# A gated linear recurrence on one Trainium2 core: scores of two levels made behind one chunk

## The chip, the cores and the metric

The kernel runs on one core of a Trainium2 chip. Its engines are TensorE (PE, matmuls; its weight loads are listed apart as PEld), VectorE (DVE), ScalarE (ACT), GpSimd (POOL) and SyncE (SP, which here issues the DMAs). Each runs its own instruction stream; streams are ordered only by semaphores. The metric is the device time of one execution in microseconds (us). The kernel before takes 2609.4 us (median of 3 runs, 2609.22 to 2610.02).

## The reference, cut to what matters

Two transformer blocks over 256 tokens of width 2048. The change touches the mixer of the first, a gated linear recurrence in both directions over 8 heads of width 128, beside a short convolution:

```python
proj = einsum('bsd,de->bse', rmsnorm(x), w_in)          # 8 pieces of 1024 columns
q_pre, fz_f, fz_b, i_pre, gate, b_gate, c_gate, h_conv = split(proj)
# per head, forward and, on flipped rows, backward (log_f: log of the forget gate, k = 1 - f):
#   S_t = diag(f_t) S_{t-1} + k_t v_t^T ;  o_t = S_t^T q_t
o = rmsnorm(o_fwd + o_bwd) * silu(gate)
y_conv = b_gate * conv3(c_gate * h_conv)
x = x + concat(o, y_conv) @ w_out
```

## The kernel before, in words

**Chunks.** Every large product streams its weights in chunks of 256 rows by 512 columns. SP loads a chunk to `raw` (a ring of 4), ACT rounds it to `hi` (L309), DVE makes the rest `lo` = `raw` - `hi` (L315), and PE multiplies it in 12 matmuls of 128x512 (L328 to L330) for two token tiles. A load waits for the `lo` four chunks before, a `hi` for PE's end of the chunk four before. PE's accumulators are two banks pairs, `acc[:, 0]` and `acc[:, 1]`; eight chunks make one block of 512 columns, which ACT then reads out (`act_scaled`, L735).

**The recurrence** runs inside 96 such chunks, in four groups of two heads (`GROUPS`), 24 chunks each (`RC`), three blocks a group: chunks 0-7 and 8-15 both into `acc[:, 0]`, 16-23 into `acc[:, 1]`. The order of everything is written by hand: each engine has a loop over g and k (`act_rec`, `dve_rec`, `pe_rec`), and steps are hung behind its own chunk k. ACT reads block 0 out behind its chunk 9 and block 1 behind its chunk 17; PE waits for the first before its chunk 8 (L1168).

**The levels.** Instead of a scan the kernel makes the 128x128 score matrix of each head and token tile in `ST` = 8 levels. Level s covers pairs of positions whose distance is decided in halves of 2^s rows. For each level:

- DVE `dve_decay(g, s)`: two products of 128x512 into `h_kd[s % 2]` and `h_qd[s % 2]` (L1001, L1003). It waits until the scores of level s - 2 are made. `dve_widen` (two more, L1009, L1011) prepares the factors of the next level, for s < 7.
- PE `scores(g, s)`: four products of 128x128 in f32, recorded as 8 matmuls (L1131), into `aux[:, s % 2]`. It waits for the decays of level s, and for the copy that empties its bank: for s = 2 to 6 the masked copy of level s - 2 by DVE (`a`), for s = 7 ACT's copy of level 5 (`kept`), for s = 0 and 1 ACT's copies of the group before.
- Copies into the matrix `h_a`: levels 0 to 4 by DVE (`dve_keep`, L989, a copy under a mask), 5 to 7 by ACT (`act_keep`, L915, L907).

PE then multiplies the matrix with the values (`output`, L1149, L1151, 16 records of 128x128) behind chunk 21 (in the last group behind 23). The same streams hold, for the next group, ACT's gate functions behind chunk 16 and keys behind 19, DVE's keys behind 17 (L962, L966) and gates behind 19 (L973), and, in the last group, the convolution (`pe_conv`, `act_conv`, `dve_conv`, L1229).

**Where the steps stand before.** PE: scores of level s behind its chunk 5 + 2s (5, 7, ..., 19). DVE: decays behind its chunks 6, 7, 9, 11, 13, 15, 16, 18, masked copies behind 8, 10, 12, 14, 16. ACT: copies of levels 5, 6, 7 behind 19, 21, 23.

Of the kernel before, what the change touches and what calls it, by code (L numbers as in the profile page):

```python
# [105 lines left out]
def build_program(nc, a, out):  # L106
    V, A, T = nc.vector, nc.scalar, nc.tensor
    with ExitStack() as ctx:
# [182 lines left out]
        g = 0  # L291
# [11 lines left out]
        def act_chunk(act, c, i, per, n=NB):  # L303

            k = c % RING
            act.wait_ge(raw_ready[k], i * (per // RING * 16) + 16 * (c // RING) + 16)
            if c >= RING or later(i):
                act.wait_ge(chunk_used, i * per + c - RING + 1)
            A.activation(hi[:, k, :, 0:n], raw[:, k, :, 0:n], ACT.Copy).then_inc(hi_ready, 1)  # L309
# [529 lines left out]
        DVE_KEEPS = 5  # L839
# [13 lines left out]
        def rec_chunk(g, k):  # L853
            return CH["in1b"] + RC * g + k
# [28 lines left out]
        def act_rec_readout(act, n):  # L883
            c0, func = REC[n // 3][n % 3]
            act.wait_ge(chunk_used, CH["in1b"] + 8 * (n + 1))
            act_scaled(act, c0, acc[:, 1 if n % 3 == 2 else 0], func).then_inc(h_sem["blk"], 1)
# [17 lines left out]
        def act_keep(act, g, s):  # L904
            act.wait_ge(h_sem["s"], g * ST + s + 1)
            if s == LEVELS:
                A.activation(h_c[:], aux[:, s % 2], ACT.Copy).then_inc(h_sem["kept"], 1)  # L907
                return
            act.wait_ge(h_sem["a"], (g + 1) * DVE_KEEPS)
            h = 1 << s  # L910
            for b in range(P // (2 * h)):
                for r, c in ((2 * b, 2 * b + 1), (2 * b + 1, 2 * b)):
                    rows_, cols_ = slice(r * h, (r + 1) * h), slice(c * h, (c + 1) * h)
                    dst = h_a[rows_].rearrange("p (x n) -> p x n", x=4)[:, :, cols_]
                    ins = A.activation(dst, aux[rows_, s % 2].rearrange("p (x n) -> p x n", x=4)[:, :, cols_], ACT.Copy)  # L915
            ins.then_inc(h_sem["kept"], 1)
# [5 lines left out]
        def act_rec(act):  # L922
            for g in range(GROUPS):
                last = g == GROUPS - 1
                for k in range(RC):
                    act_chunk(act, rec_chunk(g, k), 0, 4 * RC)
                    if k == 1:
                        if g:
                            act_rec_readout(act, 3 * g - 1)
                        else:  # L930
                            act_in1_readout(act, 3)
                    if k == 2 and g:
                        act_rec_root(act, g - 1)
                    if k == 3:
                        act_trq(act, g, 0)
                        act_trq(act, g, 1)
                    if k == 4:
                        act_trq(act, g, 2)
                    if k == 6:
                        act_rec_factors(act, g)  # L940
                    if k in (19, 21, 23):
                        act_keep(act, g, DVE_KEEPS + (k - 19) // 2)
                    if k in (9, 17):
                        act_rec_readout(act, 3 * g + (k - 9) // 8)
                    if not last:
                        if k == 16:
                            act_rec_gates(act, g + 1)
                        if k == 19:
                            act_rec_keys(act, g + 1)
                    else:  # L950
                        if k == 19:
                            act_conv(act, 0)
                            act_conv(act, 1)
                        if k in (21, 22):
                            act_conv(act, k - 19)
# [29 lines left out]
        def dve_keep(dve, cd, g, s):  # L985
            dve.wait_ge(h_sem["s"], g * ST + s + 1)
            dve.sem_inc(h_sem["alone"])
            mk = masks[:, s * P:(s + 1) * P].unsqueeze(1).to_broadcast([P, 4, P])
            cd.done(V.copy_predicated(h_a[:].rearrange("p (x n) -> p x n", x=4), mk, aux[:, s % 2].rearrange("p (x n) -> p x n", x=4)))  # L989
            dve.sem_inc(h_sem["a"])  # L990
# [61 lines left out]

        def dve_rec(dve, cd):
            cd.done(V.memset(h_a[:], 0.0))
            D_AT = {6: 0, 7: 1, 9: 2, 11: 3, 13: 4, 15: 5, 16: 6, 18: 7}
            dve.wait_ge(s_cols, 4)
            for g in range(GROUPS):
                last = g == GROUPS - 1
                for k in range(RC):
                    dve_chunk(dve, rec_chunk(g, k), 0, 4 * RC)  # L1060
                    if k == 0 and g:
                        dve_rec_norm(dve, cd, g - 1)
                    if k == 3:
                        if g in (0, 2):
                            dve_ada_keep(dve, A_IN1 + g // 2, 0)
                    if k == 4 and g:
                        dve_rec_y(dve, cd, g - 1)
                    if k == 5:
                        dve_diagonal(dve, cd, g)
                    if k >= 8 and k % 2 == 0 and k // 2 - 4 < DVE_KEEPS:  # L1070
                        dve_keep(dve, cd, g, k // 2 - 4)
                    if k in D_AT:
                        dve_decay(dve, cd, g, D_AT[k])
                        if D_AT[k] < LEVELS:
                            dve_widen(dve, cd, D_AT[k])
                    if g < 2 and k in ADA_REC[g]:
                        dve_ada(dve, cd, A_REC, 0, ADA_REC[g][k], ada_ring0)
                    if not last:
                        if k == 17:
                            dve_rec_keys(dve, cd, g + 1)  # L1080
                        if k == 19:
                            dve_rec_gates(dve, cd, g + 1)
                        if k == 23:
                            dve_copied(dve, g)
                    else:
                        if k == 7:
                            dve_conv_input(dve, 0)
                        if k == 15:
                            dve.wait_ge(h_sem["tr"], 3 * GROUPS)
                            V.memset(cv_u[:], 0.0).then_inc(cv["zero"], 1)  # L1090
                        if 19 <= k < 23:
                            dve_conv(dve, cd, k - 19)
                        if k == 23:
                            dve_conv_input(dve, 1)

        def pe_rec(pe):
# [38 lines left out]
            def output(g):  # L1135
# [15 lines left out]
                    ins = T.matmul(o, h_c[:, x4o * P:(x4o + 1) * P], vh[1 - t], start=False, stop=True)  # L1151
                ins.then_inc(h_sem["o"], 1)

            for g in range(GROUPS):
                last = g == GROUPS - 1
                pe.wait_ge(h_sem["k"], g * 2 + 2)
                if g:
                    pe.wait_ge(h_sem["copied"], g)
                transposed(g, 0)
                transposed(g, 1)  # L1160
                for k in range(RC):
                    if k == 0:
                        if g:
                            pe.wait_ge(h_sem["blk"], 3 * g - 1)
                        else:
                            pe.wait_ge(acc_free[0], 2)
                    if k == 8:
                        pe.wait_ge(h_sem["blk"], 3 * g + 1)  # L1168
                    if k == 16:
                        if g:  # L1170
                            pe.wait_ge(h_sem["blk"], 3 * g)
                        else:
                            pe.wait_ge(acc_free[1], 2)
                    pe_chunk(pe, rec_chunk(g, k), 0, 4 * RC, acc[:, k // 16], CK * (k % 8), k % 8 == 0, k % 8 == 7)
                    if k == 1:
                        if g in (0, 2):
                            if g:
                                pe.wait_ge(h_sem["kept"], g * ACT_KEEPS)
                            pe_ada(pe, A_IN1 + g // 2, 0)
                        transposed(g, 2)  # L1180
                    if k == 3:
                        gates_turned(g)
                    if 5 <= k <= 19 and k % 2:
                        scores(g, (k - 5) // 2)
                    if last:
                        if k == 16:
                            pe_conv(pe, 0)
                            pe_conv(pe, 1)
                        if k in (18, 19):
                            pe_conv(pe, k - 16)  # L1190
                    if k == (23 if last else 21):
                        output(g)
# [1350 lines left out]
```

## Time and profile before

| | |
|---|---|
| median of 3 runs | 2609.4 us |
| span of the profiled execution, first to last instruction | 2606.9 us |
| PE busy | 2587.1 us (99%) |
| DVE busy | 1825.4 us (70%) |
| ACT busy | 1414.8 us (54%) |
| recurrence, four groups | 102.4 to about 415 us of the span |
| granted TensorE clock, mean | 0.999 of 2.4 GHz |

The profile is of one execution. Its times count from the first instruction. A record's duration is from its start to its modelled end; matmuls are pipelined, so the distance of two starts, not the duration, tells what one costs. Busy and idle of an engine don't tell by themselves what sets the time: an engine that is idle beside a busy PE costs nothing.

### The profile page before, as it was taken

What the parts mean: (1) busy time and instruction counts of PE and PEld (TensorE: products, weight loads), DVE (VectorE), ACT (ScalarE), POOL (GpSimd) and SP (SyncE); (2) the same over time, 40 slices, a digit from 0 to 9 for tenths busy, and PEclk for the clock granted to TensorE, in tenths of its full rate; (3) what the DMA queues carried; (4) which work ended last, traced back from release to release, by engine and by line L of the source; (5) the groups of instructions that cost most, each with busy time, mean ns of one, the idle gap of its engine ahead of it and who ended that gap; (6) DMA issues with size and microseconds to landing.
All of it is one profiled execution on the core that took longest, in us unless ns stands there. A gap on an engine that the chain in (4) does not pass through costs nothing.

```text
span 2606.9 us, 33516 instructions
## 1 busy us (share of the span) xinstructions
PE 2587.1 (99%) x11881; PEld 2145.5 (82%) x11881; DVE 1825.4 (70%) x2168; ACT 1414.8 (54%) x1861; POOL 14.6 (1%) x28
## 2 busy tenths in 40 slices
PE   9999999999999999999999999999999999999999
PEld 7888888878888888888788888888788888888887
DVE  5888888777777878888875545566687654445565
ACT  6555545465656465445566556544465556565443
POOL 1000000000000000000000000000000000000000
PEclk9999999999999999999999999999999999999999
DMA  7765556778888888887665555555578765655554
GB/s 247 253 194 178 170 151 205 268 262 291 283 292 285 291 285 297 283 293 253 199 202 157 167 171 160 184 204 186 183 269 289 254 198 191 195 190 197 192 193 172
DMA packets 302590, 582.20 MB, mean 223 GB/s; under 512 B 20133, under 2 KB 20913, under 8 KB 302097
## 3 DMA queue, kind: packets, MB, share of 16 engines
q1 hardware_dynamic: 301008, 576.26, 66.7%
q0 software_dynamic: 1008, 3.55, 0.4%
q8 instruction: 70, 1.15, 0.2%
q10 hardware_dynamic: 464, 0.93, 0.1%
q14 instruction: 40, 0.32, 0.0%
HBM read 578.55 MB, written 2.11 MB: 223 GB/s over the span
## 4 chain that ended last, share of the span: by engine, by line
PE 95%; DVE 3%; ACT 1%; issue 1%; DMA 0%; ACTq 0%; DVEq 0%
PE acc L328 30%; PE acc L330 30%; PE acc L329 30%; DVE lo L315 1%; PE aux L1131 1%; DVE op_lo L509 0%; PE tp L482 0%; DVE op_hi L508 0%; ACT stage L494 0%; PE tp L1105 0%; PE aux L2258 0%; PE aux L2257 0%; PE tp L542 0%; DMA rows<-attn_norm_w 0%; PE tp L1151 0%
## 5 line engine op out<-in xcount | busy, mean ns | idle before, releaser
L315 DVE TENSOR_TENSOR lo<-raw,hi 128x1024 fp32r<-128x1024 f32 x895 | 1077.2, 1222 | 430.5 <-ACT hi L309 409.6
L309 ACT ACTIVATE hi<-raw 128x1024 fp32r<-128x1024 f32 x895 | 928.3, 1056 | 528.5 <-PE acc L330 368.8
L328 PE MATMUL acc<-hi,op_hi 128*128 128x512 f32 x2752 | 1084.9, 394 | 8.5 <-DVE lo L315 5.9
L330 PE MATMUL acc<-hi,op_lo 128*128 128x512 f32 x2752 | 1072.1, 390 | 0.0
L329 PE MATMUL acc<-lo,op_hi 128*128 128x512 f32 x2752 | 1071.5, 389 | 0.0
L328 PEld LDWEIGHTS acc<-hi,op_hi 128*128 128x128 f32 x2752 | 516.9, 188 | 119.6 <-issue 11.2
L330 PEld LDWEIGHTS acc<-hi,op_lo 128*128 128x128 f32 x2752 | 516.6, 188 | 109.0
L329 PEld LDWEIGHTS acc<-lo,op_hi 128*128 128x128 f32 x2752 | 517.2, 188 | 102.6
L591 DVE SCALAR_TENSOR_TENSOR ada_acc<-ada_ring,cact,ada_acc 128x512 f32<-128x512 f32 x360 | 269.5, 749 | 7.6 <-DVE small L431 0.6
L328 PE MATMUL acc<-hi,f_hi 128*128 128x512 f32 x704 | 274.5, 390 | 0.1
L329 PE MATMUL acc<-lo,f_hi 128*128 128x512 f32 x704 | 273.9, 389 | 0.0
L330 PE MATMUL acc<-hi,f_lo 128*128 128x512 f32 x704 | 273.9, 389 | 0.0
L1408 ACT ACTIVATE hid<-f_g 32x256 f32 (+1 forms) x352 | 146.3, 416 | 66.7 <-DVE f_g L1473 58.7
L1575 ACT ACTIVATE f_hi<-hid 128x512 fp32r<-128x512 f32 x88 | 55.6, 632 | 227.4 <-PE acc L330 227.4
L328 PEld LDWEIGHTS acc<-hi,f_hi 128*128 128x128 f32 x704 | 132.2, 188 | 27.8 <-issue 0.5
L330 PEld LDWEIGHTS acc<-hi,f_lo 128*128 128x128 f32 x704 | 132.2, 188 | 27.4
L329 PEld LDWEIGHTS acc<-lo,f_hi 128*128 128x128 f32 x704 | 132.2, 188 | 27.2
L1595 DVE TENSOR_TENSOR f_lo<-hid,f_hi 128x512 fp32r<-128x512 f32 x88 | 60.8, 691 | 95.3 <-ACT f_hi L1575 94.7
L735 ACT ACTIVATE proj<-acc,small 128x512 f32<-128x512 f32 x32 | 20.3, 685 | 56.0 <-PE acc L330 54.8
L508 DVE CAST op_hi<-stage 128x512 fp32r<-128x512 f32 x41 | 17.4, 425 | 42.4 <-ACT stage L494 42.2
L1849 ACT ACTIVATE proj<-acc 128x1024 f32<-128x1024 f32 x23 | 23.6, 1027 | 22.8 <-PE acc L330 22.6
L1131 PEld LDWEIGHTS aux<-h_qd,h_kd 128*128 128x128 f32 x256 | 33.5, 191 | 2.5
(336 smaller groups left out, 1284.0 us busy)
## 6 DMA issues: line engine op xcount, KB each, us to landing
raw<-w_in SPq DMA_DIRECT2D x257, 512.0 KB, 3.9
ada_ring<-w_ada SPq DMA_DIRECT2D x192, 512.0 KB, 5.3
raw<-w_gate_up SPq DMA_DIRECT2D x176, 512.0 KB, 5.2
raw<-w_ffn_in SPq DMA_DIRECT2D x176, 512.0 KB, 4.4
raw<-w_down SPq DMA_DIRECT2D x88, 512.0 KB, 5.8
raw<-w_ffn_out SPq DMA_DIRECT2D x88, 512.0 KB, 4.3
raw<-w_out SPq DMA_DIRECT2D x64, 512.0 KB, 4.1
raw<-w_proj_mla SPq DMA_DIRECT2D x16, 512.0 KB, 3.9
```

Of the source, the lines that this page charges most:

```text
L309: A.activation(hi[:, k, :, 0:n], raw[:, k, :, 0:n], ACT.Copy).then_inc(hi_ready, 1)
L315: V.tensor_tensor(lo[:, k, :, 0:n], raw[:, k, :, 0:n], hi[:, k, :, 0:n].bitcast(F32), ALU.subtract).then_inc(lo_ready, 1)
L328: T.matmul(dst, lh, hi[:, k, kk, 0:n], start=first and kk == 0, stop=False)
L329: T.matmul(dst, lh, lo[:, k, kk, 0:n], start=False, stop=False)
L330: mm = T.matmul(dst, ll, hi[:, k, kk, 0:n], start=False, stop=last and kk == CK - 1)
L591: ins = V.scalar_tensor_tensor(out=ada_acc[:], in0=ring[:, j, kk], scalar=cact[:, m:m + 1], in1=ada_acc[:], op0=ALU.mult, op1=ALU.add)
L735: ins = A.activation(proj[:, t, dst0:dst0 + NB], src[:, t], func, scale=r0[:, t:t + 1])
L1131: ins = T.matmul(aux[:, s % 2, x4 * P:(x4 + 1) * P], kd[:, x4 * P:(x4 + 1) * P], qd[:, y4 * P:(y4 + 1) * P], start=True, stop=True)
L1408: A.activation(dst, src, ACT.Copy).then_inc(f["ev"], 1)
L1575: A.activation(f_hi[:, j % 2], hid[:, 2 * kc:2 * kc + 2, :], ACT.Copy).then_inc(f["sp"], 1)
L1595: V.tensor_tensor(f_lo[:, j % 2], hid[:, 2 * kc:2 * kc + 2, :], f_hi[:, j % 2].bitcast(F32), ALU.subtract).then_inc(lo_done, 1)
L1849: A.activation(dst, acc[:, bank2(n)], func).then_inc(acc_free[bank2(n)], 1)
```

## The change

PE's scores stand in pairs: levels 0 and 1 behind its chunk 6, 2 and 3 behind 10, 4 and 5 behind 15, 6 and 7 behind 19. DVE's decays move to its chunks 6, 7, 10, 11, 14, 16, 19, 20 and its masked copies to 9, 12, 13, 15, 18. ACT's three copies move from chunks 19, 21, 23 to 20, 22, 23. No instruction is added or taken away, and each step waits for the same semaphores at the same counts.

```diff
@@ act_rec
-                    if k in (19, 21, 23):
-                        act_keep(act, g, DVE_KEEPS + (k - 19) // 2)
+                    if k in (20, 22, 23):
+                        act_keep(act, g, DVE_KEEPS + (20, 22, 23).index(k))
@@ dve_rec
-            D_AT = {6: 0, 7: 1, 9: 2, 11: 3, 13: 4, 15: 5, 16: 6, 18: 7}
+            D_AT = {6: 0, 7: 1, 10: 2, 11: 3, 14: 4, 16: 5, 19: 6, 20: 7}
+            K_AT = {9: 0, 12: 1, 13: 2, 15: 3, 18: 4}
...
-                    if k >= 8 and k % 2 == 0 and k // 2 - 4 < DVE_KEEPS:
-                        dve_keep(dve, cd, g, k // 2 - 4)
+                    if k in K_AT:
+                        dve_keep(dve, cd, g, K_AT[k])
@@ pe_rec
+            SCORES_AT = {6: 0, 10: 2, 15: 4, 19: 6}
...
-                    if 5 <= k <= 19 and k % 2:
-                        scores(g, (k - 5) // 2)
+                    if k in SCORES_AT:
+                        scores(g, SCORES_AT[k])
+                        scores(g, SCORES_AT[k] + 1)
```

## Rows read from the trace of the kernel before

**Rows 1.** The page: busy time by engine, and the chain that ended last.
```profile
PE 2587.1 (99%) x11881; PEld 2145.5 (82%) x11881; DVE 1825.4 (70%) x2168; ACT 1414.8 (54%) x1861; POOL 14.6 (1%) x28
...
PE 95%; DVE 3%; ACT 1%; issue 1%; DMA 0%; ACTq 0%; DVEq 0%
```

**Rows 2.** Waits of PE, whole run: for whom, us in total, times, longest.
```profile
PE acc L328 <- DVE lo L315: 5.9, 15, 0.8
PE acc L328 <- ACT proj L735: 1.9, 4, 0.5
```

**Rows 3.** Windows of the groups: busy by engine, granted clock (PEclk), DMA share, GB/s.
```profile
102.40:180.00 77.60, 77.14 (x391) 65.34 (x390) 66.26 (x90) 42.46 (x51) 0.96 (x1) 1.00 0.65 209
180.00:257.30 77.30, 76.83 (x389) 65.12 (x388) 66.22 (x89) 46.08 (x54) 0.95 (x1) 1.00 0.59 177
```

**Rows 4.** Timeline of PE, group 0, levels 3 and 4: start us, us, what.
```profile
141.04 1.05 PE L1131 MATMUL aux<-h_qd,h_kd 128*128 128x128 f32 x8
141.85 0.48 PE L328 MATMUL acc<-hi,op_hi 128*128 128x512 f32 x1
142.16 0.40 PE L329 MATMUL acc<-lo,op_hi 128*128 128x512 f32 x1
...
147.38 1.05 PE L1131 MATMUL aux<-h_qd,h_kd 128*128 128x128 f32 x8
```

**Rows 5.** Timeline of PE, group 1: `output`, then two chunks, then group 2's start.
```profile
250.14 0.38 PE L1149 MATMUL tp<-proj,h_a 128*128 128x128 f32 x2
...
257.38 0.60 PE L1105 MATMUL tp<-plain,h_q 128*128 128x128 f32 x4
```

**Rows 6.** Timelines of PE and ACT, group 1, around chunks 7 and 8.
```profile
198.60 1.05 PE L1131 MATMUL aux<-h_qd,h_kd 128*128 128x128 f32 x8
...
204.04 0.39 PE L330 MATMUL acc<-hi,op_lo 128*128 128x512 f32 x1
...
204.72 0.39 PE L330 MATMUL acc<-hi,op_lo 128*128 128x512 f32 x1
204.94 1.05 PE L1131 MATMUL aux<-h_qd,h_kd 128*128 128x128 f32 x8
206.46 0.50 PE L328 MATMUL acc<-hi,op_hi 128*128 128x512 f32 x1 [0.47 <-ACT proj L735]
...
212.06 1.05 PE L1131 MATMUL aux<-h_qd,h_kd 128*128 128x128 f32 x8
...
205.14 1.27 ACT L735 ACTIVATE proj<-acc,small 128x512 f32<-128x512 f32 x2 [3.93 <-PE acc L330]
```

**Rows 7.** Timelines of PE and DVE, group 0, the same place.
```profile
127.35 0.39 PE L330 MATMUL acc<-hi,op_lo 128*128 128x512 f32 x1
...
129.09 0.50 PE L328 MATMUL acc<-hi,op_hi 128*128 128x512 f32 x1 [0.47 <-ACT proj L735]
...
130.10 1.23 DVE L315 TENSOR_TENSOR lo<-raw,hi 128x1024 fp32r<-128x1024 f32 x1 [0.96 <-ACT hi L309]
```

**Rows 8.** Timeline of DVE, last group, chunks 7 and 8.
```profile
357.64 1.22 DVE L1229 TENSOR_TENSOR proj<-proj 128x1024 f32<-128x1024 f32 x1
358.78 1.22 DVE L315 TENSOR_TENSOR lo<-raw,hi 128x1024 fp32r<-128x1024 f32 x1
```

**Rows 9.** Timeline of DVE, group 1, decay of level 1, chunks 9 to 11.
```profile
199.94 0.68 DVE L1003 TENSOR_TENSOR h_qd<-h_qT,h_w 128x512 f32<-128x512 f32 x1
...
204.00 1.23 DVE L315 TENSOR_TENSOR lo<-raw,hi 128x1024 fp32r<-128x1024 f32 x1 [0.15 <-DVE h_a L989]
...
207.79 1.23 DVE L315 TENSOR_TENSOR lo<-raw,hi 128x1024 fp32r<-128x1024 f32 x1
208.93 0.73 DVE L989 COPY_PREDICATED h_a<-masks,aux 128x512 f32<-128x512 uint8 x1
209.81 1.22 DVE L315 TENSOR_TENSOR lo<-raw,hi 128x1024 fp32r<-128x1024 f32 x1 [0.15 <-DVE h_a L989]
```

**Rows 10.** Timelines of DVE and PE behind the recurrence: PE waits for `lo`.
```profile
427.58 1.22 DVE L315 TENSOR_TENSOR lo<-raw,hi 128x1024 fp32r<-128x1024 f32 x1
...
428.94 0.47 PE L328 MATMUL acc<-hi,op_hi 128*128 128x512 f32 x1 [0.37 <-DVE lo L315]
```

**Rows 11.** Timelines of ACT and DVE, group 1, chunks 16 to 19.
```profile
222.29 1.06 ACT L309 ACTIVATE hi<-raw 128x1024 fp32r<-128x1024 f32 x1 [2.57 <-PE acc L330]
...
228.95 1.04 ACT L309 ACTIVATE hi<-raw 128x1024 fp32r<-128x1024 f32 x1
...
237.03 1.29 DVE L973 SCALAR_TENSOR_TENSOR proj<-proj,h_g 128x512 f32<-128x512 f32 x2
```

**Rows 12.** Timeline of PE at the start, and the window of 5 to 10 us.
```profile
4.96 0.26 PE L699 MATMUL aux<-plain,rows 16*128 16x16 f32 x1 [4.96 <-DMA rows<-attn_norm_w]
5.14 2.93 PE L701 MATMUL acc<-plain 128*128 128x128 f32 x12
7.87 1.91 PE L482 MATMUL tp<-plain,xres 128*128 128x128 f32 x8
9.57 1.28 PE L811 MATMUL acc<-plain 128*128 128x128 f32 x8
...
5.00:10.00 5.00, 5.00 (x23) 4.96 (x24) 1.83 (x4) 2.03 (x4) 1.82 (x4) 1.00 0.97 314
```

## The prediction, made before the changed kernel was run

> **What bounds the kernel now.** I read the page's busy times and the chain that ended last first: TensorE (PE) is busy for 99% of the span and 95% of the chain is PE [rows 1]. So time is lost or won only where PE starts something later or earlier. Next the list of PE's waits: over the whole run PE waits 5.9 us for VectorE's (DVE) `lo` and 1.9 us for ScalarE's (ACT) read-out at L735, the latter in four waits of at most 0.5 us [rows 2], one in each of the four head groups that the change touches. The windows of the four groups show PE busy for 77.14 of 77.60 us in the first and alike in the others, at a granted clock of 1.00 (the 2.4 GHz level), while DVE is busy for 66 us of 77 [rows 3]. PE sets the pace; DVE is the engine with the least room. Then the timeline of PE in one group, and DVE's and ACT's beside it, because the question is which wait is hidden now and by what.
>
> **What a score block costs.** Matmuls of a chunk start 0.227 us apart (204.04 to 204.72 is three of them) [rows 6], so a chunk (12) is 2.72 us and two chunks 5.44 us. Block to block over two chunks is 147.38 - 141.04 = 6.34 us [rows 4], over five blocks on average 6.35: a block of one level (8 records) costs 6.35 - 5.44 = 0.91 us. What two levels in a row cost is not in the trace, but `output` is the same kind of work, 16 records of 128x128 f32: from its first record at 250.14 to the next group's first at 257.38 is 7.24 us, less two chunks 1.80 us [rows 5]. So a pair costs 1.80 against 2 x 0.91: **joining two blocks saves 0.02 us.** The bound above this is what can be seen of the switch, a gap of 0.31 instead of 0.227 us after the block's first following matmul [rows 4], 0.08 us; below, nothing. I take 0.02, since `output` has the very shape; three or four joins in each of four groups are 0.3 us at most (bound: 1.3 us).
>
> A page speaks for more: by the Trainium skill (TensorE: Matmul & The Clock Gate, section "What happens when you issue a matmul") a matmul that stands alone shows its drain and one in a stream hides it, a constant of 398 cycles at 2.4 GHz, 0.166 us. As an estimate from that page, 16 joins that each hide one such constant would save 2.7 us and the sum would end at 2616.3 us; the measured 1.80 against 1.82 us does not bear it out for these blocks.
>
> **What is moved: level 1 away from the read-out.** Chunks 0-7 and 8-15 of a group both accumulate in `acc[:, 0]`. So before chunk 8 PE waits until ACT has read block 0 out (L1168), and ACT can start only when chunk 7 is done. In the trace: chunk 7's last matmul starts at 204.72 (call it R), ACT's two L735 start at 205.14, chunk 8 starts at 206.46 [rows 6]. That is R + 1.74 us, whatever PE does in between, and the other groups show the same (127.35 to 129.09) [rows 7]. Now PE makes the level-1 scores in that gap and idles only 0.47 us [rows 6]. After the change they stand behind chunk 6 with level 0, and nothing stands behind chunk 7. The gap stays 1.74 us, and PE's idle share of it rises by a block, to about 1.36 us. **Lost cover: 0.90 us in each group, 3.6 us in all.** No other read-out of the recurrence is waited for (chunk 16 and the next group's chunk 0 use banks that were read long before, and PE shows no wait there).
>
> **What is newly waited for: level 3 behind chunk 10.** `scores(g, 3)` waits for `a` >= 5g + 2 (L1119, L1120), the second masked copy, because both levels use `aux` bank 1. Before, that copy was at DVE's chunk 10 and the scores at PE's chunk 11. Now the copy is at DVE's chunk 12 (K_AT) and the scores behind PE's chunk 10. Whether PE waits depends on when DVE gets there. Count from R.
> PE: chunk 8 at R + 1.74; two chunks with their start take 5.60 (206.46 to 212.06) [rows 6], the third 2.72: level 2 starts at R + 10.06, level 3 could start at R + 10.95.
> DVE: ACT issues the chunk-10 `hi` behind the read-out, so `lo` of chunk 10 comes at R + 2.75, as in group 0, where DVE waited for it (127.35 to 130.10) [rows 7]. DVE has nothing before it to delay it: in the latest group, the last, L1229 and `lo` 8 are at 357.64 and 358.78, and `lo` 9 and copy 0 (1.14 + 0.88 more) end some 2 us ahead of it [rows 8]. Then chunk 10 with its decay pair and widening takes 3.79 us (204.00 to 207.79), and so does chunk 11: `lo` 12 at R + 10.33. Copy 1 starts 1.14 later (207.79 to 208.93) and DVE is past it after 0.88 (209.81) [rows 9]: R + 12.35. From a DVE end to PE takes 0.14 (`lo` ends 428.80, PE starts 428.94) [rows 10]: R + 12.49.
> **New wait: 12.49 - 10.95 = 1.54 us**; 1.4 if the 0.15 us after the copy and the 0.14 us overlap. I take 1.5 us a group, 6.0 us in all. Behind the waiting PE instruction stand the level-3 scores, chunk 11 and all that follows; while PE stands, ACT's `hi` and DVE's `lo` of later chunks only get further ahead.
>
> **What else is moved, and what hides it.** Level 1's decay at DVE's chunk 7 is done at 200.62 (starts 199.94) [rows 9]; its scores now start at 198.60 + 2.72 + 0.90 = 202.2 [rows 4, 6], a margin of 1.6 us; no other group's is smaller. Levels 4 and 5 need decays at DVE's chunks 14 and 16 and copies 2 and 3 (chunks 13, 15): DVE reaches the last of these some 4 us before PE ends chunk 15. Levels 6 and 7 are the thinnest. ACT's gate functions keep `hi` 17 back by 6.66 us after `hi` 16 (222.29 to 228.95) [rows 11]. With chunk 11 at R + 13.3, `hi` 16 is at R + 19.0, `hi` 17 at 25.7, `lo` 17 at 26.9; the keys of the next group take DVE to R + 29.9; `lo` 18 and copy 4, 2.0; `lo` 19 and decay 6, 3.8; the next gates, 1.3 [rows 11]; `lo` 20 and decay 7's two products 2.5: R + 39.5. PE comes to level 7 at R + 27.0 (level 4) + 1.80 + 4 x 2.72 + 0.9 = R + 40.6. Margin 1.1 us: cost nothing, and 1 us a group if DVE is that much later. ACT's last copies (behind chunks 22 and 23) end about R + 43 and `output` comes at R + 47. SyncE's DMAs keep their order; GpSimd's one memset waits for decay 7 as before and has the next group's chunks 0 to 5 left. In the last group the convolution steps are behind the same decays, and DVE ends `lo` 23 some 2 us before PE wants it.
>
> **The sum.** In a group, beyond 24 chunks: before, seven blocks of 0.91 and the section with the read-out, 206.46 in its middle (204.94 to 212.06 less 5.44 = 1.68) [rows 6], 8.05 us. After, four pairs of 1.80, the same 1.68, and the wait of 1.5: 10.38 us. That is +2.33 a group, **+9.3 us** for four. PE is the bound from there to the end, and its waits for `lo` (5.9 us over the whole run [rows 2]) hang on its own pace through the ring of four chunks, so nothing gives the time back. The profiled execution has a span of 2606.9 us, 2.5 us below the median of 2609.4; the span would be 2616.2, the time **2618.7 us** (+0.36%).
>
> **The rivals.**
> (a) Only the cover is lost; level 3 doesn't wait. For it: DVE runs up to three chunks ahead and waits for PE more often than PE for it. Against: DVE must sit out the read-out too. From its `lo` 10 to the end of copy 1 it has 9.6 us of work (2 x 3.79 + 1.14 + 0.88), PE from chunk 8 to level 3 has 9.2, and PE starts 1.0 us sooner. 4 x 0.90 - 0.3 = +3.3: 2612.7 us. It needs DVE 1.5 us earlier than counted.
> (b) More waits: level 7 for decay 7, or the start after a wait dearer than the 0.34 us seen; 1 us a group for three groups: 2621.7 us.
> (c) **Faster**: a block costs because it is a block, not because of its matmuls. Place: the switch to the 128x128 f32 work and back. If the 0.91 were all fixed, before would pay seven of them a group beside the gap and after four; 4 x (3 x 0.91 - 1.5) = 4.9 us less: 2604.5 us. It decides from a fixed cost of 0.6 us a block upward. For it: each switch shows a visible step. Against: `output`, with twice the records, costs twice as much [rows 5].
> (d) The clock falls in the two pauses of a group. At the start, after 4.96 us of idle, the same kind of 128x128 records come 0.23 us apart (12 from 5.14 to 7.87) and 0.21 us (to 9.57), against 0.11 within a score block: the 1.2 GHz level, though the granted clock reads 1.00 there [rows 12]. 4.4 us at half pace lose 2.2 us; once a group 8.9: 2627.6 us. Against: the known waits of 0.47 us left the clock at 1.00 and the pace unchanged [rows 3, 6]; pauses of 1.4 and 1.5 us are shorter than the start's. The Trainium skill (same page, section "Why this matters for your kernels") warns of idle gaps between bursts for this reason; no row here has one of such a length.
>
> **How the numbers follow.** Forecast (9.3 us, both waits) 0.76; (a) 0.11; (b) 0.07; (c) 0.04; (d) 0.02. 0.2% is 5.2 us, about what a measurement of this kernel can tell from no change: slower is the forecast with (b) and (d), 0.85; within it (a) and a weak form of (c), 0.12; faster 0.03. The range reaches to (a) below, 2612.5, and to (b) above, 2621.7; terms of the forecast alone (joins up to 1.3, wait 1.4 to 1.54) give 2617.3 to 2619.
>
> **What would show it.** The wait of L328 for ACT L735 grows from 1.9 us to some 5.5 in four waits; PE's L1131 appears as waiting for DVE's masked copy (L989), four times, 1.5 us each; chunk 8 still starts 1.74 us after chunk 7's last matmul; a pair without a wait costs 1.80 us beyond its chunks; each group is 2.3 us longer; granted clock 1.00. No wait at level 3 would be (a), one at level 7 (b), a pair much under 1.8 us (c). The prediction is wrong if DVE reaches copy 1 before R + 11, or if something after the recurrence takes the delay back.

## The result

The changed kernel takes 2617.7 us (median of 6 runs, 2617.2 to 2618.3) against 2609.3 us: 8.4 us more, a ratio of 1.0034 with a 95% interval of 1.0024 to 1.0043. Run once more beside other kernels it took 2617.8 us against 2608.8, 9.0 us more (1.0021 to 1.0048). The profiled execution has a span of 2615.9 us, 9.0 us longer than that of before. The forecast was 2618.7 us, 9.3 us more, in a range of 2612.5 to 2621.7.

What PE waited for over the whole run, in the changed kernel (for whom; us in total, times, longest), answers to [rows 2]. The lines of the code have moved by one from `pe_rec` on: L1132 are the scores; at L990 DVE raises the semaphore behind a masked copy.

```profile
PE acc L328 <- ACT proj L735: 5.4, 4, 1.4
PE acc L328 <- DVE lo L315: 5.4, 14, 0.8
...
PE aux L1132 <- DVEq L990: 4.8, 4, 1.2
```

The wait for the read-out has grown from 1.9 to 5.4 us, in the same four places, and a new wait has come, of the scores for the masked copy, four times 1.2 us of idle. No other wait is new but one of 0.2 us far from the recurrence. The timeline of PE in group 1 of the changed kernel, chunks 6 to 10 with what stands behind them, answers to [rows 6]:

```profile
203.70 1.95 PE L1132 MATMUL aux<-h_qd,h_kd 128*128 128x128 f32 x16
...
208.00 0.39 PE L330 MATMUL acc<-hi,op_lo 128*128 128x512 f32 x1
209.74 0.50 PE L328 MATMUL acc<-hi,op_hi 128*128 128x512 f32 x1 [1.36 <-ACT proj L735]
...
218.06 1.05 PE L1132 MATMUL aux<-h_qd,h_kd 128*128 128x128 f32 x8
220.32 1.13 PE L1132 MATMUL aux<-h_qd,h_kd 128*128 128x128 f32 x8 [1.21 <-DVEq L990]
221.20 0.48 PE L328 MATMUL acc<-hi,op_hi 128*128 128x512 f32 x1
```

Chunk 7's last matmul starts at 208.00, chunk 8 at 209.74: 1.74 us apart, as before, but with nothing between them. Level 2 starts at 218.06; level 3 should follow 0.89 us behind, at 218.95, and comes at 220.32. DVE over the same stretch answers to [rows 9]:

```profile
206.64 0.73 DVE L989 COPY_PREDICATED h_a<-masks,aux 128x512 f32<-128x512 uint8 x1
210.67 1.23 DVE L315 TENSOR_TENSOR lo<-raw,hi 128x1024 fp32r<-128x1024 f32 x1 [3.30 <-ACT hi L309]
...
214.46 1.23 DVE L315 TENSOR_TENSOR lo<-raw,hi 128x1024 fp32r<-128x1024 f32 x1
...
218.25 1.23 DVE L315 TENSOR_TENSOR lo<-raw,hi 128x1024 fp32r<-128x1024 f32 x1
219.40 0.72 DVE L989 COPY_PREDICATED h_a<-masks,aux 128x512 f32<-128x512 uint8 x1
220.27 1.22 DVE L315 TENSOR_TENSOR lo<-raw,hi 128x1024 fp32r<-128x1024 f32 x1 [0.15 <-DVE h_a L989]
```

DVE stands idle for 3.30 us until the chunk-10 `hi`, which ACT makes behind the read-out, and then works without a break to copy 1 at 219.40. Level 1's scores were done by about 205.7, so copy 1 could have been made in that idle time; when PE wanted it, DVE was busy with other steps.

The windows of groups 0 and 1, cut at each group's first record, answer to [rows 3] (busy of PE, PEld, DVE, ACT, POOL; granted clock; DMA share; GB/s):

```profile
102.50:182.40 79.90, 77.33 (x391) 65.26 (x390) 66.09 (x90) 42.86 (x51) 0.95 (x1) 1.00 0.64 202
182.40:262.10 79.70, 77.14 (x389) 65.05 (x388) 65.96 (x89) 46.21 (x54) 0.95 (x1) 1.00 0.56 173
```

PE has nearly the same work (77.33 and 77.14 us, against 77.14 and 76.83 before) in windows that are 2.3 and 2.4 us longer, at a granted clock of 1.00.

### The profile page after: what moved, and what is told of

Same layout as the page of the kernel before. It is cut to its first block, busy times and chain, and to the rows that moved or that the text cites. A ratio compares the mean times of both kernels' runs of the same rounds, so it can differ in the third digit from the quotient of the medians.

```text
span 2615.9 us, 33513 instructions
## 1 busy us (share of the span) xinstructions
PE 2588.0 (99%) x11881; PEld 2145.2 (82%) x11881; DVE 1824.7 (70%) x2168; ACT 1415.0 (54%) x1861; POOL 14.6 (1%) x28
## 4 chain that ended last, share of the span: by engine, by line
PE 94%; DVE 5%; ACT 1%; issue 1%; DMA 0%; ACTq 0%; DVEq 0%
PE acc L328 30%; PE acc L330 30%; PE acc L329 30%; DVE lo L315 1%; PE aux L1132 1%; DVE op_lo L509 0%; PE tp L482 0%; DVE op_hi L508 0%; ACT hi L309 0%; ACT stage L494 0%; DVE h_w L1011 0%; PE tp L1106 0%; PE aux L2261 0%; PE aux L2260 0%; DVE h_w L1009 0%
## 5 line engine op out<-in xcount | busy, mean ns | idle before, releaser
L735 ACT ACTIVATE proj<-acc,small 128x512 f32<-128x512 f32 x32 | 20.3, 684 | 55.9 <-PE acc L330 54.7
L1132 PE MATMUL aux<-h_qd,h_kd 128*128 128x128 f32 x256 | 32.1, 276 | 4.8 <-DVEq L990 4.8
L1132 PEld LDWEIGHTS aux<-h_qd,h_kd 128*128 128x128 f32 x256 | 31.3, 191 | 6.7 <-issue 5.5
```

What stands on the lines that cost most here:

```text
L735: ins = A.activation(proj[:, t, dst0:dst0 + NB], src[:, t], func, scale=r0[:, t:t + 1])
L1132: ins = T.matmul(aux[:, s % 2, x4 * P:(x4 + 1) * P], kd[:, x4 * P:(x4 + 1) * P], qd[:, y4 * P:(y4 + 1) * P], start=True, stop=True)
```

## The experiments

Theory: the 9 us are two pauses of PE in each group. One is the lost cover of the read-out: 0.90 us of its gap that level 1 used to fill now stand idle. The other is the wait for copy 1, 1.5 us. Rivals: DVE is too full whatever the order of its steps; the pauses are taken back elsewhere; a score block costs as a block; the clock falls in the pauses. All times below are medians against the kernel before on the same chip; an experiment is compared with the changed kernel through them (8.4 or 9.0 us above before).

| kernel | us | against before | ratio, 95% interval |
|---|---|---|---|
| copy 1 early | 2611.8 | +2.9 | 1.0002 to 1.0021 |
| level 1 back in the gap | 2614.0 | +5.1 | 1.0011 to 1.0029 |
| before, level 1 out of the gap | 2612.6 | +3.8 | 1.0005 to 1.0023 |
| pair in the gap, copy 1 early | 2605.3 | -3.5 | 0.9978 to 0.9996 |
| the same again | 2605.3 | -3.5 | 0.9978 to 0.9996 |
| before, pair in the gap | 2606.0 | -2.8 | 0.9979 to 0.9997 |
| copy 1 later still | 2625.2 | +16.4 | 1.0048 to 1.0076 |
| copy 1 later still, pair in the gap | 2618.8 | +10.3 | 1.0027 to 1.0054 |
| changed kernel again | 2617.8 | +9.0 | 1.0021 to 1.0048 |

### Copy 1 early

```diff
-            K_AT = {9: 0, 12: 1, 13: 2, 15: 3, 18: 4}
+            K_AT = {9: 0, 10: 1, 13: 2, 15: 3, 18: 4}
```

> The changed kernel with DVE's masked copy 1 behind its chunk 10 (ahead of decay 2) and no longer behind chunk 12. Everything else as changed. Theory (two costs: lost cover 0.90 us and wait for copy 1, 1.5 us a group): copy 1 ends about 4.6 us after chunk 7's last matmul, decay 3 about 9.8, level 3 wants them at 10.95; the wait goes, 4 x 1.5 = 5.9 us less than the changed kernel, some 2.5 to 3.3 us above the kernel before; PE waits only 1.36 us for ACT L735, four times. Rival 1 (DVE is simply too full there, whatever the order of its steps): the wait turns up as one for decay 3 (L1003) and most of the 5.9 us stays. Rival 2 (the time is lost to the later levels or to the start after a pause): less than 2 us comes back.

2.9 us above before, so 5.5 to 6.1 of the 8.4 to 9.0 us are gone. The timeline of DVE in group 1 of this kernel:

```profile
208.88 1.23 DVE L315 TENSOR_TENSOR lo<-raw,hi 128x1024 fp32r<-128x1024 f32 x1 [3.30 <-ACT hi L309]
210.02 0.73 DVE L989 COPY_PREDICATED h_a<-masks,aux 128x512 f32<-128x512 uint8 x1
...
215.31 0.68 DVE L1003 TENSOR_TENSOR h_qd<-h_qT,h_w 128x512 f32<-128x512 f32 x1
```

and PE's:

```profile
207.95 0.50 PE L328 MATMUL acc<-hi,op_hi 128*128 128x512 f32 x1 [1.36 <-ACT proj L735]
216.27 1.95 PE L1132 MATMUL aux<-h_qd,h_kd 128*128 128x128 f32 x16
```

The same work in another order: decay 3 ends at 215.99, still ahead of level 3 (216.27 + 0.89), and the 16 records of levels 2 and 3 stand without a break. PE's list of waits has none for a masked copy and none for a decay. The wait was the place of copy 1, not DVE's load; rivals 1 and 2 fall.

### Level 1 back in the gap

```diff
                     if k in SCORES_AT:
                         scores(g, SCORES_AT[k])
-                        scores(g, SCORES_AT[k] + 1)
+                        if k != 6:
+                            scores(g, SCORES_AT[k] + 1)
+                    if k == 7:
+                        scores(g, 1)
```

> The changed kernel with level 1's scores behind PE's chunk 7, in the read-out's gap, and level 0 alone behind chunk 6. Theory: the cover is back, 0.90 us a group, less 0.02 for the join undone: 3.5 us less than the changed kernel, some 5 us above the kernel before. The idle before chunk 8 is 0.47 us again, and the wait for copy 1 stays at 1.2 us idle, because DVE's stretch hangs on the same read-out. Rival (the pause costs nothing by itself, DVE's lateness is all): time as the changed kernel, since the wait for copy 1 grows by what the pause gives back.

5.1 us above before, 3.3 to 3.9 below the changed kernel. PE in group 1:

```profile
206.20 1.05 PE L1132 MATMUL aux<-h_qd,h_kd 128*128 128x128 f32 x8
207.71 0.50 PE L328 MATMUL acc<-hi,op_hi 128*128 128x512 f32 x1 [0.47 <-ACT proj L735]
216.03 1.05 PE L1132 MATMUL aux<-h_qd,h_kd 128*128 128x128 f32 x8
218.28 1.13 PE L1132 MATMUL aux<-h_qd,h_kd 128*128 128x128 f32 x8 [1.20 <-DVEq L990]
```

The idle before chunk 8 is 0.47 us as in the kernel before, and the wait for copy 1 is what it was (1.20 against 1.21): the two pauses are independent, since both are counted from the same read-out. By the rival (DVE's lateness is all, so the wait for copy 1 grows by what the gap gives back) that wait would have been 2.1 us.

### The kernel before, level 1 out of the gap

```diff
-                    if 5 <= k <= 19 and k % 2:
-                        scores(g, (k - 5) // 2)
+                    if (5 <= k <= 19 and k % 2 and k != 7) or k == 6:
+                        scores(g, 1 if k == 6 else (k - 5) // 2)
```

> The kernel before with one step moved: level 1's scores behind PE's chunk 6 and not behind 7. No pairs, no other step moved. Theory: the read-out's gap stays 1.74 us from start to start and PE idles 1.36 us of it: 0.91 us a group, 3.6 us above the kernel before. Rival (PE would use the pause otherwise, ACT's read-out begins sooner with an idle TensorE): under 1.5 us above.

3.8 us above before: one block moved by one chunk, with no pair made. Its profile has PE waiting 5.4 us for L735 in four waits, as the changed kernel's. This is the lost cover by itself.

The traces show the two costs side by side, without the rest of the run. From the first group's first record to the last group's first `output` record it is 310.7 us before, 320.0 in the changed kernel, 314.1 with copy 1 early, 316.3 with level 1 back in the gap, and 314.3 here. So the wait for copy 1 is 5.9 us and the cover 3.6 to 3.7.

### The pair in the gap

```diff
-            K_AT = {9: 0, 12: 1, 13: 2, 15: 3, 18: 4}
+            K_AT = {9: 0, 10: 1, 13: 2, 15: 3, 18: 4}
...
-            SCORES_AT = {6: 0, 10: 2, 15: 4, 19: 6}
+            SCORES_AT = {7: 0, 10: 2, 15: 4, 19: 6}
```

> The changed kernel with two steps moved: the pair of levels 0 and 1 stands behind PE's chunk 7, inside the read-out's gap, and copy 1 behind DVE's chunk 10. Theory: a pair reaches from 0.23 to 1.93 us after chunk 7's last matmul, the read-out is done at 1.74; PE waits nowhere. In a group 1.80 us stand where the kernel before had 0.91 + 1.68: 0.79 less, and three joins 0.06: 4 x 0.85 = 3.4 us below the kernel before (2606.0 us). Rival (a block costs as a block): four pairs a group at 0.91 instead of seven blocks and the gap, 3 us a group less, some 15 us below. Rival (DVE falls behind because copy 0 comes after its wait for level 0): a wait for decay 2 or copy 1, gain under 1 us.

3.5 us below the kernel before, and 12.5 below the changed kernel (each against the kernel before), with two numbers of the changed kernel altered. PE and ACT in group 1:

```profile
203.26 0.39 PE L330 MATMUL acc<-hi,op_lo 128*128 128x512 f32 x1
203.49 1.95 PE L1132 MATMUL aux<-h_qd,h_kd 128*128 128x128 f32 x16
205.19 0.48 PE L328 MATMUL acc<-hi,op_hi 128*128 128x512 f32 x1
...
203.68 1.26 ACT L735 ACTIVATE proj<-acc,small 128x512 f32<-128x512 f32 x2 [3.02 <-PE acc L330]
```

Chunk 8 starts 1.93 us after chunk 7's last matmul, without a wait; the read-out ends at 204.94, some 0.25 us before that. The whole gap is work. PE's list of waits has no L735 and no L990 in it. The time agrees with the theory's 0.85 us a group (3.4 us in all) and not with a block that costs as a block, which would have made it some 15 us.

> The kernel with the pair of levels 0 and 1 in the gap and copy 1 behind DVE's chunk 10 once more, beside the one that has only the pair in the gap. Theory: 3.4 us below the kernel before, and 0.2 us or nothing below its neighbour, which lacks three joins a group.

The second run of this kernel gives 2605.3 us again.

### The kernel before with that pair alone

```diff
-                    if k >= 8 and k % 2 == 0 and k // 2 - 4 < DVE_KEEPS:
+                    if k == 9:
+                        dve_keep(dve, cd, g, 0)
+                    if k > 8 and k % 2 == 0 and k // 2 - 4 < DVE_KEEPS:
                         dve_keep(dve, cd, g, k // 2 - 4)
...
-                    if 5 <= k <= 19 and k % 2:
+                    if k == 7:
+                        scores(g, 0)
+                    if 7 <= k <= 19 and k % 2:
                         scores(g, (k - 5) // 2)
```

> The kernel before with level 0's scores moved from behind PE's chunk 5 into the gap behind chunk 7, ahead of level 1, and copy 0 from DVE's chunk 8 to 9; levels 2 to 7 one by one as before. Theory: 1.80 us where 0.91 + 1.68 stood, 0.79 a group: 3.2 us below the kernel before. The kernel with all four pairs (3.5 us below) has three more joins a group and can be 0.2 us better at most. Rival (a join is worth what the step in the stream shows, 0.08 us and more): the four pairs are better by 1 us or more, so this one comes out at most 2.5 us below.

2606.0 us, 2.8 us below before. The four-pair kernel is 0.74 us better, between the two expectations. The traces are finer: from the first group's first record to the last group's first `output` record it is 307.52 us here and 307.39 with four pairs, 0.13 us for twelve joins, 0.01 us each. Most of the rest stands behind the recurrence, where the two kernels do the same: from that record to the end it is 2194.3 us here and 2193.7 in both traces of the four pairs. Over all eleven traces of this case that stretch takes 2193.4 to 2194.5 us, so a difference of half a microsecond of the whole time can't be put down to the recurrence. The runs of the two kernels overlap too (2605.0 to 2606.6 and 2604.9 to 2606.0).

### Copy 1 later still

```diff
-            K_AT = {9: 0, 12: 1, 13: 2, 15: 3, 18: 4}
+            K_AT = {9: 0, 13: 2, 15: 3, 18: 4}
...
+                    if k == 13:
+                        dve_keep(dve, cd, g, 1)
                     if k in K_AT:
```

> The changed kernel with DVE's masked copy 1 behind its chunk 13 (just ahead of copy 2) and no longer behind chunk 12, so that one more lo (1.14 us) stands before it. Theory: the wait for copy 1 grows by that 1.14 us in each group, from 1.37 to 2.5 us; 4.6 us above the changed kernel, 13 us above the kernel before. Rival (the wait has slack in it, or PE's later stretch takes part of it back): clearly less than 4.6 us more.

Neither the theory nor the rival foresaw this: 16.4 us above before, 7.4 above the changed kernel, where 4.6 or less were expected. The wait did grow as the theory says, by 1.16 us of idle. PE in group 1:

```profile
224.20 1.17 PE L1134 MATMUL aux<-h_qd,h_kd 128*128 128x128 f32 x8 [2.37 <-DVEq L990]
225.09 0.72 PE L328 MATMUL acc<-hi,op_hi 128*128 128x512 f32 x1
225.60 0.63 PE L329 MATMUL acc<-lo,op_hi 128*128 128x512 f32 x1
226.03 0.63 PE L330 MATMUL acc<-hi,op_lo 128*128 128x512 f32 x1
...
228.16 0.58 PE L329 MATMUL acc<-lo,op_hi 128*128 128x512 f32 x1
228.59 0.40 PE L330 MATMUL acc<-hi,op_lo 128*128 128x512 f32 x1
228.82 0.40 PE L328 MATMUL acc<-hi,op_hi 128*128 128x512 f32 x1
```

and windows of the same place (granted clock third from the end):

```profile
224.00:225.00 1.00, 0.80 (x7) 0.83 (x8) 0.73 (x1) 0.00 (x0) 0.00 (x0) 1.00 0.96 334
225.00:226.00 1.00, 1.00 (x5) 0.84 (x5) 0.85 (x2) 0.00 (x0) 0.00 (x0) 0.58 1.05 393
226.00:227.00 1.00, 1.00 (x4) 0.78 (x3) 1.00 (x3) 0.00 (x0) 0.00 (x0) 0.50 0.61 229
...
229.00:230.00 1.00, 1.00 (x6) 0.79 (x6) 0.00 (x0) 0.23 (x1) 0.00 (x0) 1.00 0.42 160
```

The granted clock is still 1.00 when PE goes on at 224.20 and falls behind 225. The matmuls then come 0.43 us apart instead of 0.23, for about 3.5 us, at a granted clock of 0.50: the 1.2 GHz level. That costs 1.6 us (from level 2 to level 4 it is 19.6 us here and 18.0 us in group 2, where it did not happen). In the profiled execution it happened in three of the four groups: 4.8 us. With the 4.6 of the longer waits this is 9.4 us; from the first group to the last `output` it is 9.3 longer than in the changed kernel's second profile (329.2 against 319.9), and the span is 9.8 longer. The runs spread from 2624.0 to 2627.7 us, as they would if one to three groups were hit. Only one execution has a trace, but the mean granted clock that each run has on record goes the same way, as far as its three digits tell: 0.998 in the two longest (2627.1 and 2627.7), 0.999 in the other three, and never below 0.999 in any run of the kernel before or the changed one.

### The long pause alone

The kernel just shown, with the pair in the gap:

```diff
-            SCORES_AT = {6: 0, 10: 2, 15: 4, 19: 6}
+            SCORES_AT = {7: 0, 10: 2, 15: 4, 19: 6}
```

> The kernel with the late copy 1 (behind DVE's chunk 13), with the pair of levels 0 and 1 moved into the read-out's gap, so that the pause before chunk 8 is gone and the pause for copy 1 (about 2.2 us of idle) stands alone. Question: does the clock fall seen with the late copy need both pauses of a group, or the long one alone? If no clock falls: 1.8 us a group below what the late copy would take at full clock (2622.4 us), 2615.1 us, all matmuls 0.23 us apart. If the long pause alone is enough: stretches of 0.43 us from start to start behind some of the four waits for copy 1, 1.6 us for each, 2616.7 to 2621.5 us, and executions that differ by steps of 1.6 us.

2618.8 us (2616.6 to 2620.6). The clock still falls: in the profiled execution, the fastest of the five with 2616.6 us, behind one of four pauses, in group 2.

```profile
300.00:302.00 2.00, 2.00 (x6) 1.57 (x5) 2.00 (x4) 0.00 (x0) 0.00 (x0) 0.50 0.57 208
```

That execution is the 2615.1 us of the sum and one fall of 1.6. The other four runs are longer and have a mean granted clock of 0.998 on record, against 0.999 for this one. So one pause of 2.2 us can be enough. None of the pauses of 0.5 to 1.4 us in any profile here had such a stretch behind it: in all eleven the granted clock reads 1.00 up to the last matmul, but for the four stretches named.

### The changed kernel again

> The changed kernel itself, beside the other two on one chip. Theory: 8 to 9 us above the kernel before; the profiled execution has the two waits, 1.36 us of idle for the read-out and 1.21 us for copy 1, four times each.

9.0 us above before, with 1.36 and 1.21 us of idle as in the first profile.

## Why the prediction was right

**The bound.** PE's pace carried through: from the first group's first record to the last group's first `output` record the recurrence takes 310.7 us before and 320.0 us after, 9.3 us more. The span is 9.0 us longer. The stretch from that `output` to the end is 0.4 us shorter (2193.4 against 2193.8), but it varies by 1.1 us among the traces, so this doesn't show that the delay was taken back; "nothing gives the time back" stands to within that.

**The blocks.** A pair was put at 1.80 us. In group 1 of the changed kernel levels 4 and 5 start at 234.94 and levels 6 and 7 at 247.62; less four chunks of 2.72 that is 1.80 us. A join is worth 0.01 to 0.02 us. The estimate from the Trainium skill (TensorE: Matmul & The Clock Gate, section "What happens when you issue a matmul"), a drain of 0.166 us hidden in each join, would have made it 2.0 us for twelve joins; the traces gave 0.13 us. Rival (c) was rightly held small.

**The cover.** Forecast 0.90 us a group, 3.6 in all. Measured by itself 3.8 us in the medians and 3.6 in the trace, idle 1.36 us as written, chunk 8 at R + 1.74 to the hundredth. Rival (a), this cost alone at 2612.7 us, is nearly the kernel with copy 1 early: 2611.8.

**The wait.** Counted as 1.54 us, taken as 1.5. The counted times, from chunk 7's last matmul, R = 208.00: `lo` 10 at R + 2.75, measured 2.67; level 2 at R + 10.06, measured 10.06; copy 1 at R + 11.47, measured 11.40; PE on at R + 12.49, measured 12.32. So level 3 came 1.37 us late, 0.17 less than counted. Some 0.1 of that is the overlap that the forecast named and did not take ("1.4 if the 0.15 us after the copy and the 0.14 us overlap"): from the start of copy 1 to PE it is 0.92 us, counted as 1.02. The whole cost, from level 2 to level 4 (218.06 to 234.94 less five chunks and a pair), is 1.48 us. The 0.11 us between is the slower start after a pause (the block's 8 records take 1.13 instead of 1.05 us), which the forecast left out. That the two errors nearly cancel is luck; the mechanism is not. The list of waits shows 1.21 us of idle each time and not the 1.5 written as a sign, because idle counts from a record's modelled end (1.05 us behind level 2's start, where the next block could start after 0.89). Moving copy 1 forward gave 5.5 to 6.1 us back (5.9 in the traces) of 6.0 forecast.

**What was hidden.** In group 1 level 1's decay ended 1.6 us before its scores, as counted. Decay 7 ends at 247.2 and level 7 is due at 248.5: a margin of 1.3 us against 1.1 counted. Rival (b) did not come.

**The clock.** Rival (d) did not come in the changed kernel: granted clock 1.00, no stretch of a slower pace. But it was nearer than its chance of 0.02 says. 1.2 us more of the same wait brought it, and at 1.6 us a time, not the 2.2 worked out from the start of the kernel. The forecast's reason against it (the pauses are shorter than the 5 us of the start) gave no bound.

**The size.** 9.3 us forecast, 8.4 and 9.0 measured; 9.0 in the spans and 9.3 in the recurrence alone. The differences are of the size of what the rest of the run varies by.

## What to carry to other kernels

Before steps are gathered, look for what they stood in front of: a small block between two chunks may be free because the engine would wait there anyway, and the place is worth more than the joining (0.9 us against 0.02). Gathering two steps behind one point also makes the second one due earlier; count its supplier from the same event (here the read-out that holds both engines) and put the supplier's step right behind the supplier's own pause, ahead of work that isn't due yet, as with copy 1 early. The same steps put into the gap, not ahead of it, made the kernel faster than it was.

## What the runs showed of the hardware

A pause of TensorE of 2.2 to 2.4 us inside dense work can bring its clock down to the 1.2 GHz level for about 3.5 us, at 1.6 us a time, in some groups and not in others of one execution: three of four (2.37 us of idle, with one of 1.35 us that ended some 9 us ahead) and one of four (2.21 us alone). The clock fell not in the pause but 0.6 to 1.5 us after the matmuls had gone on (224 to 225 us still reads 1.00, though PE went on at 224.20). Pauses of up to 1.4 us did so in none of the profiles. Nothing between 1.4 and 2.2 us was run, and why one group was hit and not another is open. The Trainium skill (TensorE: Matmul & The Clock Gate, section "HAM oscillation — how this bites in real kernels") tells of such falls between bursts of matmuls; the traces agree that they exist, and show them behind pauses of 2.2 and 2.4 us, shorter than the waits of some 3 to 5 us in that section's case.

At the kernel's start matmuls run at half the pace after 4.96 us of idle while the granted clock reads 1.00 [rows 12]; behind the pauses in the middle of the run the clock column and the pace agree.
